# Attention stage of a two-layer trunk step: page numbers read ahead, a sorting network in place of repeated top-eights

## The reference

```python
def dsa_prompt(q, k, v, qi, ki, wi):          # 256 queries, 256 keys
    isc = indexer_scores(qib, ki, wib)        # sum over 16 heads of relu(qi . ki) * wi
    isc = jnp.where((s_pos[None, :] <= tb[:, None])[None], isc, -jnp.inf)
    vals, sel = lax.top_k(isc, 64)
    return sparse_attend(qb, gather_rows(k, sel), gather_rows(v, sel), jnp.isfinite(vals))

def dsa_sample(q, k, v, qi, ki, wi, ck, cv, cki, page_table):   # 32 queries, 1024 + 4 keys each
    ki_past = cki[page_table].reshape(DB, past, D_IDX)
    isc = indexer_scores(qi, jnp.concatenate([ki_past, ki], axis=1), wi)
    isc = jnp.where(adm[None], isc, -jnp.inf)
    vals, sel = lax.top_k(isc, 256)
    kg = jnp.where(is_past, ck[phys, off], gather_rows(k, new_i))      # pages by page_table
    vg = jnp.where(is_past, cv[phys, off], gather_rows(v, new_i))
    return sparse_attend(q, kg, vg, jnp.isfinite(vals))
```

## Time and profile before

| | |
|---|---|
| median of 3 runs | 1470.28 us (1467.61 to 1473.64) |
| profiled execution, span from first to last instruction | 1474.8 us |
| PE busy | 1406.1 us, 95% |
| DVE busy | 1088.5 us, 74% |
| ACT busy | 329.9 us, 22% |
| POOL busy | 359.9 us, 24% |
| DMA | 233.14 MB, mean 158 GB/s |
| mean granted TensorE clock | 0.968 |

### The profile page before, as it was taken

The page is one execution under the profiler, slowest core; times in us unless marked ns, Lnnn a source line. Parts: engine busy times, 40 slices in busy tenths (PEclk is TensorE's granted clock), DMA queues, the critical chain, the costliest instruction groups (busy, mean ns, idle before and its releaser), DMA issues.

```text
span 1474.8 us, 28290 instructions
## 1 busy us (share of the span) xinstructions
PE 1406.1 (95%) x11458; PEld 1291.0 (88%) x11458; DVE 1088.5 (74%) x1392; ACT 329.9 (22%) x653; POOL 359.9 (24%) x304
## 2 busy tenths in 40 slices
PE   6999999999878998999999999999999999999997
PEld 6999999995433886999999999999996669999997
DVE  7977686767976647788768597769578677787764
ACT  3111102003244432321110221110202452211110
POOL 2533212000630021443321253321200003533210
PEclk9999999999997999999999999999999879999998
DMA  8443542664876203554436344345161305344142
GB/s 310 150 171 114 185 166 91 222 211 157 279 287 249 71 4 118 197 197 170 143 124 227 132 163 159 140 145 206 72 225 59 149 33 221 143 171 165 54 160 89
DMA packets 62699, 233.14 MB, mean 158 GB/s; under 512 B 9003, under 2 KB 18545, under 8 KB 45581
## 3 DMA queue, kind: packets, MB, share of 16 engines
q1 hardware_dynamic: 50426, 224.56, 42.7%
q10 hardware_dynamic: 11554, 6.37, 1.5%
q0 software_dynamic: 624, 0.87, 0.2%
HBM read 225.54 MB, written 6.10 MB: 157 GB/s over the span
## 4 chain that ended last, share of the span: by engine, by line
PE 51%; DVE 5%; ACT 1%; DMA 1%; POOL 1%; issue 1%; DVEq 0%; POOLq 0%; SPq 0%
PE psum L191 15%; PE psum L193 15%; PE psum L192 15%; DVE pair_hi L177 1%; DMA ring<-in_w_gu 1%; DVE ring_r L186 1%; DVE x L393 1%; PE psum L235 1%; PE psum L236 1%; DVE hidden_hi L389 1%; PE psum L240 1%; DVE rstd L297 1%; POOL hidden L305 0%; POOL hidden L307 0%; PE psum L351 0%
## 5 line engine op out<-in xcount | busy, mean ns | idle before, releaser
L191 PE MATMUL psum<-x_hi_r,pair_hi 128*128 128x288 f32 x1736 | 516.3, 297 | 6.0 <-DVE up L598 2.7
L193 PE MATMUL psum<-x_hi_r,ring_r 128*128 128x288 f32 x1736 | 515.0, 297 | 0.0
L192 PE MATMUL psum<-x_lo_r,pair_hi 128*128 128x288 f32 x1608 | 474.8, 295 | 0.0
L186 DVE TENSOR_TENSOR ring_r<-ring,pair_hi 128x2048 fp32r<-128x2048 f32 (+1 forms) x127 | 340.2, 2679 | 4.3
L191 PEld LDWEIGHTS psum<-x_hi_r,pair_hi 128*128 128x128 f32 x1736 | 328.8, 189 | 8.6 <-issue 8.1
L193 PEld LDWEIGHTS psum<-x_hi_r,ring_r 128*128 128x128 f32 x1736 | 328.2, 189 | 0.0
L192 PEld LDWEIGHTS psum<-x_lo_r,pair_hi 128*128 128x128 f32 x1608 | 303.4, 189 | 0.3
L191 PE MATMUL psum<-hidden_hi_r,down_hi 128*128 128x288 f32 x704 | 208.4, 296 | 0.0
L192 PE MATMUL psum<-hidden_r,down_hi 128*128 128x288 f32 x704 | 207.7, 295 | 0.0
L193 PE MATMUL psum<-hidden_hi_r,down_r 128*128 128x288 f32 x704 | 207.0, 294 | 0.0
L177 DVE CAST pair_hi<-ring 128x2048 fp32r<-128x2048 f32 (+1 forms) x126 | 161.7, 1283 | 11.8 <-DMA ring<-in_w_gu 10.4
(11 more groups left out here) (547 smaller groups left out, 1856.8 us busy)
## 6 DMA issues: line engine op xcount, KB each, us to landing
ring<-in_w_gu SPq DMA_DIRECT2D x88, 1024.0 KB, 4.8
down<-in_w_down SPq DMA_DIRECT2D x64, 704.0 KB, 4.3
ring<-in_w_ab SPq DMA_DIRECT2D x18, 1024.0 KB, 5.2
ring<-in_w_cd SPq DMA_DIRECT2D x12, 1024.0 KB, 6.2
ring<-in_cache_k SPq DMA_DIRECT2D x32, 256.0 KB, 4.6
index_keys<-in_cache_k SPq DMA_DIRECT2D x32, 256.0 KB, 5.1
index_keys<-in_cache_i ACTq DMA_DIRECT2D x64, 64.0 KB, 2.7
eight_pages_ds<-in_cache_v SPq DMA_DIRECT2D x16, 256.0 KB, 4.8
```

The costliest lines, as they stand in the source:

```text
L186: return eng.tensor_tensor(lo, a, hi.bitcast(F32), ALU.subtract)
L191: pe.matmul(out, w_hi, x_hi, start=start, stop=False)
L192: pe.matmul(out, w_hi, x_lo, start=False, stop=False)
L193: return pe.matmul(out, w_lo, x_hi, start=False, stop=stop)
```

## The change

1. SP reads the page numbers of sequences 0 and 1 between the last two loads of projection weights, those of 2 and 3 behind V1, and those of 4 to 7 (32 reads) behind V0. K1 is loaded ahead of K2 and K3. V4 and V5 come whole behind V2 and V3.
2. The sample's value projection `values_in(2)` moves from behind the index scores into the eight rounds of prompt index scores, its ACT copy with it.
3. The first prompt tile (tokens 0 to 127) uses 128 instead of 256 keys in the prompt's index scores, their relu, accumulation and top-64.
4. `key_scores(0)` moves from behind head 2 to behind the scores of head 1; the eight copies of sample queries go from DVE to ACT.
5. The 33 rounds of `top_eight` and the old merge become a sorting network (bitonic, with alternating signs from a new 128 KB table `signs`, which POOL loads): 36 levels of one max and one min on half the columns each, then a join of the quarters and eight merge levels. `STEPS` spreads them over the heads, 18 levels between heads 1 and 2. The new keys' scores enter only in `threshold`, which gets longer by some ten small instructions. `threshold` stands behind head 5 and `select` behind head 6.

```diff
-ROUNDS = (6, 10, 14, 26, 28, 31, 33, 33, 33)
+LEVELS = tuple((m, m >> e) for m in (1 << i for i in range(8)) for e in range(m.bit_length()))
+SORTED = len(LEVELS)
+STEPS = (4, 8, 26, 32, SORTED + 1, SORTED + 5, SORTED + 9, SORTED + 9, SORTED + 9)
+SEEN = (P, TP)
@@ sync
             send_pair_loop(c, sp, stream, RING, 3)
-            send_pairs(c, sp, stream, 16, 2)
+            sp.wait_ge(idx.table_loaded, 16)
+            idx.read_numbers(sp, c, 0)
+            send_pairs(c, sp, stream, 16, 1)
+            idx.read_numbers(sp, c, 1)
+            send_pairs(c, sp, stream, 17, 1)
...
-            sp.wait_ge(idx.table_loaded, 16)
-            idx.read_numbers(sp, c, 0, 1, 2, 3)
             sp.wait_ge(c.pair_done, first + npairs)
             load("cache_k", 0, KEY_SLOTS[0])
             load("cache_v", 1, VALUE_SLOTS[1])
-            idx.read_numbers(sp, c, 4, 5)
+            idx.read_numbers(sp, c, 2, 3)
+            sp.wait_ge(c.pair_done, first + npairs + 2)
+            load("cache_k", 1, KEY_SLOTS[1])
             for u in range(4):
                 sp.wait_ge(S["is_sum"], 3 * u + 2)
                 load("cache_k", 2 + u // 2, KEY_SLOTS[2 + u // 2], range(4 * (u % 2), 4 * (u % 2) + 4))
             sp.wait_ge(S["is_used"], 12)
-            sp.wait_ge(c.pair_done, first + npairs + 2)
-            load("cache_k", 1, KEY_SLOTS[1])
             load("cache_v", 0, VALUE_SLOTS[0])
+            idx.read_numbers(sp, c, 4, 5)
             idx.read_numbers(sp, c, 6)
             idx.read_numbers(sp, c, 7)
...
-                for b in range(2, 6):
+                for b in (2, 3):
                     load("cache_v", b, VALUE_SLOTS[b], range(4 * u, 4 * u + 4))
+            for b in (4, 5):
+                load("cache_v", b, VALUE_SLOTS[b])
@@ gpsimd
+            pool.wait_ge(S["qi_done"], 1)
+            pool.wait_ge(S["ip_sum"], 16)
+            pool.dma_start(signs, c.ins["signs"]).then_inc(S["q_moved"], 16)
@@ tensor
-                        p_ = (i + t) % 2
-                        mm = pe.matmul(B[(2 * i + t) % 4][:, e * TP:(e + 1) * TP], qz_src[half(p_), 2 * (i // 2) + e, t * P:(t + 1) * P],
-                                       ki[half(p_), 0:TP], start=True, stop=True)
+                        p_, w = (i + t) % 2, SEEN[t]
+                        mm = pe.matmul(B[(2 * i + t) % 4][:, e * w:(e + 1) * w], qz_src[half(p_), 2 * (i // 2) + e, t * P:(t + 1) * P],
+                                       ki[half(p_), 0:w], start=True, stop=True)
...
                 values_in(1, range(n, n + 1))
+                values_in(2, range(n, n + 1))
                 if n < 7:
                     index_scores(n + 1)
...
             weigh(11)
-            values_in(2, range(KT))
...
+                if h == 1:
+                    key_scores(0)
                 if h == 7:
                     key_scores(1)
...
-                if h == 2:
-                    key_scores(0)
@@ scalar
             value_rows(1)
+            value_rows(2)
...
-            value_rows(2)
+            act.wait_ge(S["qz_zero"], 2)
+            for h in range(HP):
+                for p_ in range(2):
+                    last = act.activation(qz[half(p_), :, h, (2 * h + p_) * TS:(2 * h + p_) * TS + TS],
+                                          q[half(p_), h, TP:NT].rearrange("p (b t) -> p b t", t=TS), ACT.Copy)
+            last.then_inc(S["qz_done"], 1)
@@ vector
-            def top_eight(i):
-                if i:
-                    dve.wait_ge(S["ts_rep"], i)
-                dve.max(sq[:, 8 * i:8 * i + 8], wq).then_inc(S["ts_max"], 1)
-                if i < QW // 8 - 1:
-                    dve.wait_ge(S["ts_max"], i + 1)
-                    dve.match_replace(out=wq, in_to_replace=sq[:, 8 * i:8 * i + 8], in_values=wq, imm_value=TAKEN).then_inc(S["ts_rep"], 1)
+            def level(i):
+                m, d = LEVELS[i]
+                a, b = (wq, sq) if i % 2 == 0 else (sq, wq)
+                av, bv = (x.rearrange("p (n e d) -> p n e d", e=2, d=d) for x in (a, b))
                 if i:
+                    dve.wait_ge(S["ts_max"], i)
+                for e, op in enumerate((ALU.max, ALU.min)):
+                    if d == m:
+                        last = dve.scalar_tensor_tensor(bv[:, :, e], av[:, :, 1], -1.0, av[:, :, 0], ALU.mult, op)
                     else:
+                        last = dve.tensor_tensor(bv[:, :, e], av[:, :, 0], av[:, :, 1], op)
+                last.then_inc(S["ts_max"], 1)
...
-            for i in range(ROUNDS[0]):
-                top_eight(i)
-            sample_queries()
+            sorting(0, STEPS[0])
+            rk.last_tokens(dve)
+            dve.memset(newest[:, 8:16], TAKEN)
             for h in range(8):
-                if h == 7:
-                    threshold()
                 head(h)
-                for i in range(ROUNDS[h], ROUNDS[h + 1]):
-                    top_eight(i)
-                    if i == ROUNDS[h] + 1:
-                        norm(h)
-                if ROUNDS[h] == ROUNDS[h + 1]:
+                if STEPS[h] == STEPS[h + 1]:
                     norm(h)
+                else:
+                    sorting(STEPS[h], STEPS[h] + 2)
+                    norm(h)
+                    sorting(STEPS[h] + 2, STEPS[h + 1])
                 if h >= 3 and h % 2:
                     out((h - 3) // 2)
                 if h == 5:
-                    merge_quarters()
-            select()
+                    threshold()
+                if h == 6:
+                    select()
```

More of the change, by code:

```diff
@@ L1539, in dsa_stage @@
         quarters = z[:, 10:16].rearrange("p a t -> p (a t)")
-        iq, wq, sq = (quarters[:, i * QW:(i + 1) * QW] for i in range(3))
-        moved, pa_, pb_ = (quarters[:, 3 * QW + i * KS:3 * QW + (i + 1) * KS] for i in range(3))
+        iq = quarters[:, 0:QW]
+        wq, sq, moved, pa_, pb_ = (quarters[:, QW + i * KS:QW + (i + 1) * KS] for i in range(5))
+        signs = moved
+        least, newest = (quarters[0:NS, QW + 5 * KS + 16 * i:QW + 5 * KS + 16 * i + 16] for i in range(2))
         n_above, n_equal, kth = (sb(n, [NS, 1]) for n in ("n_above", "n_equal", "kth"))
@@ L1992, in vector @@
                         dve.wait_ge(S["tp_rep"], n - 1)
-                    dve.max(t8[:, t], work[:, t]).then_inc(S["tp_max"], 1)
+                    dve.max(t8[:, t], work[:, t, 0:SEEN[t]]).then_inc(S["tp_max"], 1)
                     n += 1
@@ L1996, in vector @@
                     dve.wait_ge(S["tp_max"], n - 1 + t)
-                    dve.match_replace(out=work[:, t], in_to_replace=t8[:, t], in_values=work[:, t], imm_value=TAKEN).then_inc(S["tp_rep"], 1)
+                    seen = work[:, t, 0:SEEN[t]]
+                    dve.match_replace(out=seen, in_to_replace=t8[:, t], in_values=seen, imm_value=TAKEN).then_inc(S["tp_rep"], 1)
             dve.wait_ge(S["tp_rep"], n)
@@ L2000, in vector @@
             dve.tensor_tensor(mp[:, :, :], work[:, :, :], cmask[:, :, :], ALU.add).then_inc(S["mp_done"], 1)
-            def sample_queries():
-                dve.wait_ge(S["qz_zero"], 2)
-                rk.last_tokens(dve)
-                for h in range(HP):
-                    for p_ in range(2):
-                        last = dve.tensor_copy(qz[half(p_), :, h, (2 * h + p_) * TS:(2 * h + p_) * TS + TS],
-                                               q[half(p_), h, TP:NT].rearrange("p (b t) -> p b t", t=TS))
-                last.then_inc(S["qz_done"], 1)
             def head(h):
@@ new lines, in join_quarters, with merge_level @@
+            def join_quarters():
+                dve.wait_ge(S["ts_max"], SORTED)
+                dve.tensor_copy(moved[quarter(0)], wq[quarter(1)])
+                ln(dve.tensor_copy(moved[quarter(2)], wq[quarter(3)]))
+                dve.scalar_tensor_tensor(pa_[quarter(0)], moved[quarter(0)], -1.0, wq[quarter(0)], ALU.mult, ALU.max)
+                dve.scalar_tensor_tensor(pa_[quarter(2)], wq[quarter(2)], -1.0, moved[quarter(2)], ALU.mult, ALU.min).then_inc(S["ts_max"], 1)
+            def merge_level(i):
+                d = KS >> (i + 1)
+                a, b = (pa_, pb_) if i % 2 == 0 else (pb_, pa_)
+                av, bv = (x.rearrange("p (n e d) -> p n e d", e=2, d=d) for x in (a, b))
+                dve.wait_ge(S["ts_max"], SORTED + 1 + i)
+                dve.tensor_tensor(bv[0:96, :, 0], av[0:96, :, 0], av[0:96, :, 1], ALU.max)
+                dve.tensor_tensor(bv[0:96, :, 1], av[0:96, :, 0], av[0:96, :, 1], ALU.min).then_inc(S["ts_max"], 1)
@@ L2063, in threshold, with sorting @@
+            def sorting(i0, i1):
+                for i in range(i0, i1):
+                    if i < SORTED:
+                        level(i)
+                    elif i == SORTED:
+                        join_quarters()
+                    else:
+                        merge_level(i - SORTED - 1)
             def threshold():
-                dve.wait_ge(S["ts_max"], QW // 8 + 1)
+                dve.wait_ge(S["ts_max"], SORTED + 9)
```

(14 more changed lines are left out.)

41 lines of the change are left out of this document (15 added, 26 removed).

## The result

| | before | after |
|---|---|---|
| median of 19 runs each | 1471.27 us (1467.61 to 1484.72) | 1484.78 us (1476.93 to 1492.46) |
| ratio, 95% interval | | 1.0066 (1.0046 to 1.0086) |
| profiled execution, span | 1474.8 us | 1488.1 us |
| mean granted TensorE clock | 0.968 | 0.961 |

The change costs 0.66%, 9.7 us of 1471. The table's medians lie further apart, by 13.5 us, and the means of the same runs by 10.5; single executions of one kernel scatter by 15 to 17 us, so I go by the ratio. The two profiled executions differ by 13.3 us, but not all of that belongs to the change: behind the mask products, where it changes little more, the second trace runs 8.6 to 9 us behind the first until 1042 us (before) and 1051 us (after), and loses another 4 to 5 in a later stretch that no part of the change touches.

What follows compares the result with a forecast made beforehand. PE, busy 95% of the span, bounds the kernel, so the start of the mask products decides: 453.8 - 442.7 = +11.1 us, plus 1 for the clock, on 1470.3 gives 1482. Forecast 1477 to 1490; stated range 1471 to 1489.

Steps and rivals of the forecast that it cites:

- Index scores 4.5 us later, nothing from the shorter tile: PE up to head 0: sample's index scores end at 378.1 instead of 373.6; tile 0's halved columns gain nothing, at most 2 us.
- SP: Page loads: 32 reads take 17.7 us, so K4 starts at 403.3, 4.2 us later than before.
- passes one instruction for each of POOL's 27: DVE's sort beside POOL's mixing: 25 instructions, 12.5 levels, get through by 412.1, putting head 2 at 416.
- my second reading: DVE's sort: both instructions of a level pass in one gap, POOL slowed by 5.4 us, head 2 at about 414.
- The old merge rows of 1.07 and 1.10 us: DVE instructions at 418.10 and 419.20 in the earlier trace, read as each getting through once between two of POOL's.
- the forecast's mark: Signs on DVE: levels of 2.3 us between heads 1 and 2 during mixing, 0.52 behind it; tensor-tensor instructions about 1.1 us.
- From head 2 to the last head's probabilities: Attention tail: remaining heads, join, threshold, select and head 7 take 32.9 us, so the last probabilities are ready at 448.9.
- PE's clock: PE, idle some 4 us before head 7, runs slower behind it: up to 3 us longer, 1 taken.
- Rival 1: POOL disturbs DVE's levels little and late pages decide: mask products at 445.9, +3.2 us, 1473.5; 28%.
- Rival 2: Neither POOL nor SP holds: K4 starts at about 388, levels undisturbed, -11 us, 1459; 10% with weaker forms.

Runs made afterwards that it cites:

- E9: Changed kernel with POOL's mixing begun at 365 us, beside the rounds of the prompt's top 64; ratio 1.0012 against the kernel before.
- E3: Changed kernel with 16 of the page numbers ahead of K4 read behind V1 instead; ratio 1.0051 against the kernel before.
- E4: Changed kernel with POOL's mixing held back until the last merge level of the sort; ratio 1.0051 against the kernel before.
- E11: Changed kernel with the edits of E9, E10 and E3 together; ratio 0.9972 against the kernel before.
- E10: Changed kernel with only DVE's order changed: levels spread over the heads, threshold and select behind head 7, out(2) inside the select; ratio 0.9998 against before.
- E1: Changed kernel with its sort put back to the rounds of max8 and the old threshold and select order; ratio 1.0016 against the kernel before.
- E5: Changed kernel with DVE's select put back behind head 7's maximum and reciprocal; ratio 1.0057 against the kernel before.
- E7: E6 with the edits of E3 and E5; ratio 1.0036 against the kernel before.
- E6: Changed kernel with POOL's mixing moved to 341 us, beside the prompt's index scores; ratio 1.0100 against the kernel before.

## Why the prediction was right, point by point

**The forecast** was 1482 us, 12 over the median. The measured median is 1484.8, and the ratio gives 1471.3 + 9.7 = 1481.0. The chain was the right one; its terms were not all right, and two errors partly cancel.

- **Index scores 4.5 us later, nothing from the shorter tile.** Weighing ends at 378.15 and head 0 starts at 378.38 (forecast 378.3). The index products are still eight records in 1.13 us, as in the earlier trace rows (the prediction speaks of a round's four products, which stand there as x8). The first key scores waited for K3 until 386.81, where about 384 was forecast; nothing hung on it.
- **SP.** K4 at 402.69, forecast 403.3; the 32 reads took 17.9 us, forecast 17.7, 0.56 each. By the floor of about 600 ns that the Trainium skill gives (DMA: Bandwidth & Descriptors, section "Latency and other measured facts") they would have taken an estimated 19.2; the trace's figure went before it rightly.
- **The term that was mis-sized: "passes one instruction for each of POOL's 27".** It passes two, a whole level, and POOL is slowed: 1.29 us a level instead of 2.3, and 31.2 us of mixing instead of 28.7. That was my second reading, with 1.37 us and head 2 at 414. Its sum was off as well: from 383.5, 20 levels of 1.37 and about 1 us for head 1's maximum come to 412. Head 2 came at 410.94, below my 413 to 419, since POOL gave way by 2.5 us and not by 5.4. The old merge rows of 1.07 and 1.10 us had misled me: there the first instruction had 256 elements, and each filled a gap alone; that this is the reason is not shown. Of the forecast's mark, the levels of 2.3 us are refuted. The tensor-tensor of about 1.1 us is right for one instruction of each level and wrong for the other, as one level shows (times in ns: shortest, median, longest):

```profile
L2061 DVE TENSOR_TENSOR z<-z x2: 279/643/1007, 399.4 to 400.3; 128x128 f32<-128x128 f32 x2
```

  The one that starts at 399.4 takes 1.01 us, until POOL's instruction is over (399.11 to 400.28 in POOL's timeline); the next passes in 0.28. Row 420.23 of before (0.28 us, behind the 1.10 of 419.20) had the same look, but POOL had already finished there.
- **From head 2 to the last head's probabilities** 32.9 us were forecast; 34.7 went by (410.94 to 445.60), since three more levels behind head 2 were still beside the mixing (two of them in 1.99 us from 412.16). Then 5.7 us to the mask products, forecast 4.9 and 1 for the clock. Sum 451.30, forecast 453.8 (454.8 with the clock).
- **PE's clock.** PE's wait of 4.18 us was forecast as 4, and the clock behind it fell, as windows of after (first three) and of before (last two) show; the last three columns are clock, DMA share and GB/s.

```profile
440.00:445.00 5.00, 1.42 (x8) 0.64 (x6) 3.56 (x8) 1.75 (x6) 0.00 (x0) 1.00 1.02 373
445.00:450.00 5.00, 4.40 (x16) 2.62 (x16) 0.42 (x1) 3.96 (x9) 0.00 (x0) 0.66 1.04 385
450.00:455.00 5.00, 4.42 (x13) 2.42 (x12) 1.48 (x3) 3.19 (x6) 0.00 (x0) 0.77 1.06 387
```
```profile
440.00:445.00 5.00, 4.01 (x11) 2.18 (x10) 3.00 (x6) 4.07 (x7) 0.00 (x0) 0.78 1.02 381
445.00:450.00 5.00, 4.42 (x7) 1.77 (x6) 1.84 (x4) 0.00 (x0) 0.00 (x0) 0.50 1.05 387
```

  Before is the slower one in the mask products themselves (4.04 us against 2.71 for the first six), so what the clock cost ahead of them (5.7 us instead of 4.9) it gave back there.
- **The rivals.** Rival 1 (pages decide, +3.2) is what E9 does, where fewer levels are held: mask products at 447.2. Rival 2's early K4 exists in E3, and the free levels in E4, but neither does it alone: E3 lacks the levels, and E4's mixing comes too late. E11, with both in part, gives 4 us where rival 2 had 11.

**What I missed** lies in the order. The forecast took head 2, threshold, select and head 7 as a chain that any stretching lengthens, and E10 shows that the same stretched levels cost nothing when six of them stand behind a head and the threshold and select behind the last. So "POOL holds the levels" is half of the cause: the other half is that 18 of them stood between heads 1 and 2, and the select ahead of head 7. That the number came out so near is in part luck: head 2 was forecast 5 us late, and 1.8 us too little went from there to the last head's probabilities. Where the sum of DVE's work is concerned, the network saved nothing measurable: in before, DVE was not what the mask products waited for but for 1 us.

The rule of the Trainium skill (SBUF — State Buffer, section "Who interferes with whom") is that two inputs in SBUF contend with a GpSimd instruction that reads SBUF, and one operand does not unless it is a copy or tensor-scalar in a 2-port mode. These rows agree, with the levels at 1.29 us beside the mixing and 0.52 away from it; the 1.03 us tensor-scalar of E1 fits, though no run shows its mode. The outcome is this case's: 1.29 us a level for DVE, and 0.13 us more for each of POOL's long ones.

## What to carry to other kernels

Before work on Vector is swapped for another kind, look at what GpSimd does in the same stretch and count operands in SBUF: 23 us of levels in place of 37 us of rounds became 40 where they met (busy time of the groups of after: 27.1 + 8.1 us of levels and 4.5 of merge). An in-order engine that serves a pipeline should have the pipeline's steps first and its own long job in the gaps, and a copy that waits for a later product goes inside that job, not ahead of it (worth 1 us in E5 and E7). And a faster part is worth what others wait for its engine: here 1 us.

## What the runs showed of the hardware that I had not expected

- A tensor-scalar of two elements takes 0.17 us alone and up to 1.03 us beside POOL's mixing; a copy of 128x512 from SBUF 0.43 alone and 1.21 in E6. Max8, match-replace and reduce kept 0.44, 0.42 and 0.68 us beside the same work.
- Two short DVE instructions, one behind the other, pass for one of POOL's: the first is held (1.01 us instead of 0.28), the second is not (0.28). POOL's grew by 0.13 us each (1.04 to 1.17). Beside one long instruction, the scan of 2.33 us, both grew: the scan to 3.19, POOL's from 1.18 to 3.11.
